# Fused transformer block: GpSimd forms the gated rough reciprocal of the second attention, VectorE's normalisation has three instructions instead of four

## What is computed

```python
def mla_mixer(h, cos, sin, w_in, q_norm, w_q_b, kv_norm, w_kv_b, w_out):
    u = h @ w_in
    c_q, c_kv, k_rope, z = split(u)
    q = rmsnorm(c_q, q_norm) @ w_q_b        # 16 heads of 64 + 32
    kv = rmsnorm(c_kv, kv_norm) @ w_kv_b    # 16 heads of 64 (keys) + 64 (values)
    ...
    for blk in range(S // 128):
        s = (q_nope . k_nope + q_rope . k_rope) * scale, causal by chunks of 64
        prob = softmax(s)
        outs.append(prob . v)
    o = concatenate(outs)
    return (o * silu(z)) @ w_out
```

## Time and profile before

| | |
|---|---|
| median of 3 runs (lowest, highest) | 2193.37 us (2192.48, 2194.1) |
| profiled execution: its time, its span | 2191.03 us, 2189.2 us |
| mean granted TensorE clock | 0.972 |
| busy, share of the span | PE 94%, DVE 49%, ACT 31%, POOL 48% |
| chain that ended last, by engine | PE 74%, DVE 11%, issue 6%, ACT 4%, POOL 3% |
| MLA attention | 16 steps and the last head, from about 1550 to 1953 us |

### The profile page before, as it was taken

The page is one execution under the profiler, slowest core; times in us unless marked ns, Lnnn a source line. Parts: engine busy times, 40 slices in busy tenths (PEclk is TensorE's granted clock), DMA queues, the critical chain, the costliest instruction groups (busy, mean ns, idle before and its releaser), DMA issues.

```text
span 2189.2 us, 26361 instructions
## 1 busy us (share of the span) xinstructions
PE 2053.5 (94%) x9488; PEld 1655.3 (76%) x9488; DVE 1070.3 (49%) x1189; ACT 672.8 (31%) x1085; POOL 1040.6 (48%) x651
## 2 busy tenths in 40 slices
PE   5999989989999999999999997999899999989996
PEld 3777767877778878878878875887677778768775
DVE  6545554646531211212111258422777888763576
ACT  3345564132221001001000122112466666650312
POOL 1545555423733543543443364333456655653372
PEclk9999999988999999999999998999899999999997
DMA  3100000102211211211111122111000000011122
GB/s 138 50 20 21 20 10 29 49 30 106 96 39 48 72 53 48 67 57 48 54 61 48 48 79 76 39 50 39 30 20 19 19 29 19 19 39 48 39 77 96
DMA packets 31642, 106.65 MB, mean 49 GB/s; under 512 B 3449, under 2 KB 3641, under 8 KB 31577
## 3 DMA queue, kind: packets, MB, share of 16 engines
q1 hardware_dynamic: 27520, 96.14, 13.3%
q10 hardware_dynamic: 4066, 9.74, 1.2%
HBM read 101.51 MB, written 4.26 MB: 48 GB/s over the span
## 4 chain that ended last, share of the span: by engine, by line
PE 74%; DVE 11%; issue 6%; ACT 4%; POOL 3%; ACTq 0%; DVEq 0%; DMA 0%; POOLq 0%
PE ps L225 53%; PE ps L390 4%; PE ps L242 2%; PE ps L254 2%; POOL probs_lo L686 2%; PE ps L630 2%; PE ps L618 1%; PE ps L631 1%; DVE mx L731 1%; DVE h_lo L371 1%; PE ps L637 1%; PE ps L617 1%; PE ps L616 1%; DVE tmp L1777 1%; DVE x L1779 1%
## 5 line engine op out<-in xcount | busy, mean ns | idle before, releaser
L1949 POOL TENSOR_TENSOR w_hi<-w_raw,zero 128x1024 fp32r<-128x1024 f32 (+2 forms) x173 | 322.5, 1864 | 815.7 <-PE ps L225 579.5
L1951 POOL TENSOR_TENSOR w_lo<-w_raw,w_hi 128x1024 fp32r<-128x1024 f32 (+2 forms) x173 | 421.1, 2434 | 13.6
L225 PE MATMUL ps<-h_hi,w_lo 128*128 128x512 f32 x1328 | 333.3, 393 | 5.5 <-DVE x L517 5.1
L225 PE MATMUL ps<-h_hi,w_hi 128*128 128x512 f32 x1328 | 328.0, 389 | 0.0
L225 PE MATMUL ps<-h_lo,w_hi 128*128 128x512 f32 x1216 | 300.4, 389 | 0.0
L225 PEld LDWEIGHTS ps<-h_hi,w_lo 128*128 128x128 f32 x1328 | 248.4, 189 | 60.3 <-issue 9.7
L225 PEld LDWEIGHTS ps<-h_hi,w_hi 128*128 128x128 f32 x1328 | 249.2, 188 | 51.8
L686 POOL TENSOR_TENSOR probs_lo<-probs,mla_p_hi 128x512 fp32r<-128x512 f32 x192 | 191.3, 1016 | 171.2 <-ACT probs L679 169.3
L225 PEld LDWEIGHTS ps<-h_lo,w_hi 128*128 128x128 f32 x1216 | 228.2, 188 | 47.6
L1391 DVE TENSOR_TENSOR tmp<-ps,tmp 128x1024 f32<-128x1024 f32 x22 | 26.9, 1224 | 370.3 <-PE ps L225 363.6
L731 DVE TENSOR_REDUCE mx<-ps 128x1 f32<-128x128 f32 (+1 forms) x192 | 140.9, 755 | 79.0 <-PE ps L662 44.4
(11 more groups left out here) (342 smaller groups left out, 3709.2 us busy)
## 6 DMA issues: line engine op xcount, KB each, us to landing
w_raw<-in_wpack SPq DMA_DIRECT2D x173, 512.0 KB, 3.3
x<-in_xT ACTq DMA_DIRECT2D x16, 512.0 KB, 7.9
out<-result SPq DMA_DIRECT2D x8, 512.0 KB, 2.9
p_raw<-in_pT ACTq DMA_DIRECT2D x1, 1024.0 KB, 4.8
pos_i<-in_pos SPq DMA_DIRECT2D x1, 512.0 KB, 6.3
const_stage<-in_consts SPq DMA_DIRECT2D x1, 404.0 KB, 3.3
vec<-in_vecs SPq DMA_DIRECT2D x1, 284.0 KB, 4.7
mla_q_hi<-c_neg ACTq DMA_DIRECT2D x16, 4.0 KB
```

The lines of the kernel that those rows point to most:

```text
L225: last = nc.tensor.matmul(dst[:, half, :], w[slot][:, kt, :], a[:, i, t], start=(n == 0), stop=(n == total - 1))
L1949: nc.gpsimd.tensor_tensor(w_hi[s][:, kts, :], raw[s][:, kts, :], no_change[:, kts, :], ALU.add).then_inc(w_hi_done, 1)
L1951: nc.gpsimd.tensor_tensor(w_lo[s][:, kts, :], raw[s][:, kts, :], w_hi[s][:, kts, :].bitcast(F32), ALU.subtract)\
```

## The change

1. In MLA, GpSimd computes `rec` = `r` times silu(z) (`gate_pool`), once for each half of each head: behind its low part of piece 6 for the first half and behind that of piece 11 for the second. It waits for its own low part, for `r`, and, before it goes on, for its own product.
2. VectorE's normalisation has three instructions in both attentions: sum times `r`, then (that minus 2) times `rec` in MLA (times `r` in fox), then times the output. The second of them waits for GpSimd's product in MLA.
3. `NORM_BEHIND` puts the three behind the fifth, sixth and seventh maximum. For fox this moves its first instruction from behind the fourth to behind the fifth and its second from the fifth to the sixth.
4. `r` of an odd head lies in rows 64 to 127 instead of 0 to 63, so that it stands on the rows of silu(z).

```diff
-        NORM_BEHIND = {3: (0,), 4: (1,), 5: (2,), 6: (3,)}
+        NORM_BEHIND = {4: (0,), 5: (1,), 6: (2,)}
+        GATE_AFTER = {6: 0, N_PIECES - 1: 1}
...
-            nc.scalar.activation(r0[0:HD, :], ln_sum[0:HD, :], ACT.Exp, scale=-1.0).then_inc(A.r0_done, 1)
+            nc.scalar.activation(r0[HD * b:HD * b + HD, :], ln_sum[0:HD, :], ACT.Exp, scale=-1.0).then_inc(A.r0_done, 1)
+
+        def gate_pool(pool, A, n, b, half, tile, g):
+
+            pool.wait_ge(A.p_lo_done, n * N_PIECES + (g + 3))
+            pool.wait_ge(A.r0_done, n * 2 + (half + 1))
+            rows = slice(HD * b, HD * b + HD)
+            z = flat(mix[rows, bass.ds(tile, 1), half * HALF:(half + 1) * HALF])
+            nc.gpsimd.tensor_tensor(rec[rows, :], r0[rows, :], z, ALU.mult).then_inc(A.gate_done, 1)
+            pool.wait_ge(A.gate_done, n * 2 + (half + 1))
...
             if part == 0:
                 dve.wait_ge(A.r0_done, n * 2 + (half + 1))
-                nc.vector.tensor_tensor(sums, sums, r0[0:HD, :], ALU.mult).then_inc(A.newton, 1)
+                nc.vector.tensor_tensor(sums, sums, r0[rows, :], ALU.mult).then_inc(A.newton, 1)
             elif part == 1:
                 dve.wait_ge(A.newton, seq + 1)
-                if again and not gate:
+                if gate:
+                    dve.wait_ge(A.gate_done, n * 2 + (half + 1))
+                elif half == 1 or not (isinstance(n, int) and n == 0):
                     dve.wait_ge(A.norm_done, n * 2 + half)
-                nc.vector.scalar_tensor_tensor(sums if gate else factor, sums, -2.0, r0[0:HD, :], ALU.add, ALU.mult).then_inc(A.newton, 1)
-            elif part == 2 and gate:
+                nc.vector.scalar_tensor_tensor(rec[rows, :], sums, -2.0, (rec if gate else r0)[rows, :], ALU.add, ALU.mult)\
+                    .then_inc(A.newton, 1)
+            elif part == 2:
                 dve.wait_ge(A.newton, seq + 2)
-                if again:
-                    dve.wait_ge(A.norm_done, n * 2 + half)
-                nc.vector.tensor_tensor(factor, sums, dst, ALU.mult).then_inc(A.newton, 1)
-            elif part == 3:
-                dve.wait_ge(A.newton, seq + count)
-                nc.vector.scalar_tensor_tensor(dst, out, -1.0, factor, ALU.mult, ALU.mult).then_inc(A.norm_done, 1)
+                nc.vector.scalar_tensor_tensor(dst, out, -1.0, rec[rows, :], ALU.mult, ALU.mult).then_inc(A.norm_done, 1)
...
                         for g in range(N_PIECES):
                             low_pool(pool, A, n - 1, g)
+                            if A is mla and g in GATE_AFTER:
+                                gate_pool(pool, A, n - 1, 1 - b, GATE_AFTER[g], turn - (b == 0), g)
...
                 for g in range(N_PIECES):
                     low_pool(pool, A, A.heads - 1, g)
+                    if A is mla and g in GATE_AFTER:
+                        gate_pool(pool, A, A.heads - 1, 1, GATE_AFTER[g], last, g)
```

More of the change, by code:

```diff
@@ L554, in __init__ @@
                 self.newton = sem(f"{k}_newton")
+                self.gate_done = sem(f"{k}_gate_done")
                 self.norm_done = sem(f"{k}_norm_done")
@@ L687, in low_pool, with rough_act @@
                 .then_inc(A.p_lo_done, 1)
-        def rough_act(act, A, n, half):
+        def rough_act(act, A, n, b, half):
             act.wait_ge(A.pv_done, n * N_PIECES + (LAST_OF_HALF[half] + 1 + 4))
@@ L695, in rough_act @@
             act.wait_ge(A.ln_done, n * 2 + (half + 1))
-            nc.scalar.activation(r0[0:HD, :], ln_sum[0:HD, :], ACT.Exp, scale=-1.0).then_inc(A.r0_done, 1)
+            nc.scalar.activation(r0[HD * b:HD * b + HD, :], ln_sum[0:HD, :], ACT.Exp, scale=-1.0).then_inc(A.r0_done, 1)
[6 more added lines that the diff above has]
+            pool.wait_ge(A.gate_done, n * 2 + (half + 1))
         def norm_half_dve(dve, A, n, b, half, tile, gate, part):
-            count = 3 if gate else 2
-            seq = n * (2 * count) + half * count
+            seq = n * 4 + half * 2
             rows = slice(HD * b, HD * b + HD)
@@ L704, in norm_half_dve @@
             dst = flat(mix[rows, bass.ds(tile, 1), half * HALF:(half + 1) * HALF])
-            factor = rec[rows, :] if gate else rec[0:HD, :]
-            again = half == 1 or not (isinstance(n, int) and n == 0)
             if part == 0:
                 dve.wait_ge(A.r0_done, n * 2 + (half + 1))
-                nc.vector.tensor_tensor(sums, sums, r0[0:HD, :], ALU.mult).then_inc(A.newton, 1)
+                nc.vector.tensor_tensor(sums, sums, r0[rows, :], ALU.mult).then_inc(A.newton, 1)
             elif part == 1:
                 dve.wait_ge(A.newton, seq + 1)
-                if again and not gate:
+                if gate:
+                    dve.wait_ge(A.gate_done, n * 2 + (half + 1))
+                elif half == 1 or not (isinstance(n, int) and n == 0):
                     dve.wait_ge(A.norm_done, n * 2 + half)
-                nc.vector.scalar_tensor_tensor(sums if gate else factor, sums, -2.0, r0[0:HD, :], ALU.add, ALU.mult).then_inc(A.newton, 1)
-            elif part == 2 and gate:
+                nc.vector.scalar_tensor_tensor(rec[rows, :], sums, -2.0, (rec if gate else r0)[rows, :], ALU.add, ALU.mult)\
+                    .then_inc(A.newton, 1)
+            elif part == 2:
                 dve.wait_ge(A.newton, seq + 2)
-                if again:
-                    dve.wait_ge(A.norm_done, n * 2 + half)
-                nc.vector.tensor_tensor(factor, sums, dst, ALU.mult).then_inc(A.newton, 1)
-            elif part == 3:
-                dve.wait_ge(A.newton, seq + count)
-                nc.vector.scalar_tensor_tensor(dst, out, -1.0, factor, ALU.mult, ALU.mult).then_inc(A.norm_done, 1)
+                nc.vector.scalar_tensor_tensor(dst, out, -1.0, rec[rows, :], ALU.mult, ALU.mult).then_inc(A.norm_done, 1)
         def norm_whole_dve(dve, *which):
-            for part in range(4):
+            for part in range(3):
                 norm_half_dve(dve, *which, part)
@@ L822, in step_act @@
                 if g == 6 and prev is not None:
-                    rough_act(act, A, prev, 0)
+                    rough_act(act, A, prev, 1 - b, 0)
             if prev is not None:
-                rough_act(act, A, prev, 1)
+                rough_act(act, A, prev, 1 - b, 1)
             max_row_act(act, A, n, b, turn)
@@ L835, in last_act @@
                     split(g - (N_PIECES - 2))
-            rough_act(act, A, A.heads - 1, 1)
+            rough_act(act, A, A.heads - 1, 1, 1)
             if split is not None:
```

2 lines of the change are left out of this document (1 added, 1 removed).

## The result

| | before | after |
|---|---|---|
| median of 19 runs each, same chip | 2192.86 us (2188.09 to 2196.9) | 2197.34 us (2195.2 to 2201.68) |
| ratio | | 1.0022, 95% interval 1.0016 to 1.0029 |
| profiled execution, span | 2191.03, 2189.2 us | 2197.77, 2196.0 us |
| VectorE, GpSimd busy | 1070 and 1041 us | 1048 and 1082 us |

The change makes the kernel slower by 3.5 to 6.4 us, 4.5 by the medians. The prediction had the direction, but its +10.0 is more than twice the size.

A forecast was written before the change was run, and what follows sets the result against it. The prediction took TensorE, waiting at each MLA step's end for GpSimd's last low part, as the bound. Terms 7.6 + 0 + 0 + 0.3 + 2.1 = +10.0 us on the median 2193.37 gave 2203, range 2195 to 2208.

The forecast's parts named there:

- What bounds the kernel: At an MLA step's end, TensorE's last value matmul already waits for GpSimd's low part of piece 11.
- both arms: GpSimd's low part of piece 11 and VectorE's eighth maximum, said to arrive together in odd steps; GpSimd has 0.25 room in even.
- Part 1: GpSimd's first-half product behind piece 6: takes 1.27, makes piece 7 0.80 late and piece 11 0.62 late; +7.6 us.
- the dearer case: Rival: product at 1.5 or dear waits, piece 8's low part late too, TensorE stalls twice a step; +13 to +16, chance 0.13.
- 8 x 0.62 + 7 x 0.37 = +7.6: Loss in MLA steps from GpSimd's lateness: 0.62 us in each of 8 odd steps, 0.37 in each of 7 even.
- Part 2: VectorE's first half in MLA: four instructions become three, but the eighth maximum is not earlier; 0.
- at the same distance from the fifth: Sign of being right: the eighth maximum keeps its distance from the fifth maximum in MLA steps.
- Part 3: Second half in MLA: the product, the split queued behind it and VectorE's earlier normalisation change nothing; 0.
- Part 4: Fox: the first normalising instruction moves behind the fifth maximum, idle ahead of the seventh swallows most; +0.3 us.
- Part 5: Last head and behind it: the split queues behind the product, collides with VectorE's low parts of `mix`, TensorE waits; +2.1 us.
- VectorE was the bound: Rival: VectorE's second-half work sets the step time, so 15 x 0.72 = 10.8 us would go: 2182.6; chance 0.04.
- The half-time product: Rival: GpSimd's product on half the partitions takes 0.65, steps cost 0, the end about 1.3; +1.6 us, 2195, chance 0.12.

The follow-up runs named there:

- run 4: Kernel after, with VectorE's three first-half instructions behind the fourth to sixth maximum instead of the fifth to seventh: 2195.93 us, ratio 1.0018.
- run 5: Kernel before, with only the first half's fourth normalising instruction moved from behind the seventh to behind the eighth maximum: 2185.5 us, ratio 0.997.
- run 7: Kernel before, with all four first-half instructions one maximum later, behind the fifth to eighth, and no product on GpSimd: 2194.03 us, ratio 1.0005.
- run 1: Kernel after, but MLA's first half normalised by VectorE alone with four instructions as before; GpSimd multiplies only for the second half: 2193.27 us, ratio 1.0005.
- run 2: Kernel after, but the last MLA head's second half normalised by VectorE alone, without GpSimd's product there: 2195.68 us, ratio 1.0014.
- run 9: Kernel after, last head's second half normalised by VectorE alone, but GpSimd still makes an unused product (r0 times r0) there: 2196.62 us, ratio 1.0019.
- run 3: Kernel after, with one more GpSimd product (r0 times r0) ahead of the first half's product in every MLA head: 2215.47 us, ratio 1.0107.

## Why the prediction was right or wrong

- **What bounds the kernel: this is the step that failed.** I wrote that in the odd step both arms arrive together and that TensorE's last value matmul waits for GpSimd. Lateness did pass one for one from there to the value transposes, but the step did not end by them. I took 0.94, the distance from the value transposes to the transpose of the maxima, for TensorE's own; it is 0.80. And I read the room at the transpose and not at the next step's first matmul, where the odd step has 0.38 more of it. The room was 0.45 and 0.56, where I had 0.25 and 0.
- **Part 1, the product.** 1.29 for 1.27, waits of 0.27 and 0.16 for 0.22 and 0.15, piece 7 0.91 late for 0.80, piece 11 0.68 for 0.62: right and slightly small. The new wait for piece 7's low part was not in the sum (the dearer case had one, for piece 8's), though it makes 0.55 of TensorE's 0.68. **The term "8 x 0.62 + 7 x 0.37 = +7.6" was mis-sized**: between the first matmuls of steps an even step lost 0.24 and an odd one 0.31, where I had 0.37 and 0.62, and all 15 intervals lost 3.9. GpSimd's arm alone is 2.1 of it; the rest is the late eighth maximum (run 4). So the +3.9 comes in about equal parts from the arm that I named and from the one that I had ruled out.
- **Part 2**, the eighth maximum is not earlier for the instruction that goes: right, and runs 4, 5 and 7 show why: it was the wrong one of four. But "at the same distance from the fifth" is wrong: 6.14 before, 6.46 after in the odd step.
- **Part 3**, 0 for the second half: right (run 1).
- **Part 4**, fox +0.3: 0.6, as 0.2 in every other interval and nothing in the rest. In those the gap of the earlier trace rows swallowed less.
- **Part 5**, +2.1 with 0.32 of it in the last head: the tail cost 2.0 and the last head 0.2. Runs 2 and 9 show the cause: the split behind the product, which then stands beside VectorE's low parts.
- **The rivals.** "VectorE was the bound" had 0.04 and a wrong place: not the second half, but the eighth maximum, which the chain of waits named. The first evidence of the profile was right, and I argued it away with a second view. That the time still came out in the stated range is luck in part: the sum was more than twice the loss, and half of the steps' loss has a cause that it did not hold. The half-time product is out at 1.29.

## What to carry to other kernels

Before a step is said to be ended by one engine, take the same distance in several places: the shortest one seen is the most that the engine's own work can need, and what a step has above it is room. Where a chain of waits names an engine, look for what of that engine's work can go behind the thing awaited; that needed one changed number here and gave 7 us, while taking an instruction over to another engine gave nothing. A helping engine with "50% load" is not free in the place that matters, and what its queue holds behind the new work is late too, and so is what the engine that waits for it delivers to a third.

## What was not expected of the hardware

- **The branch is paid from the wait on.** At the loop's end the next matmul came 0.51 to 0.52 behind the end of the maximum that TensorE had waited for, wherever the other work stood (before, after, run 4); at the half-way point without a branch it was 0.14. Behind step 1, where TensorE enters the loop and does not jump back, it was 0.24 (1577.49 to 1577.73 in before). That the branch itself takes the time is read from this; no run changed it alone.
- **An operand used twice is cheaper on GpSimd**: r0 times r0 took 1.04 us (runs 3 and 9), r0 times z 1.29, the same 64 x 512. Where the second operand lies differs too, so that it is the double use is likely and not shown.
- **In the tail VectorE pays, not GpSimd.** In the kernel before the split's two instructions took 2.87 and 2.38, in the kernel after 1.90 and 3.25; together 5.25 and 5.15. GpSimd loses nothing by moving, VectorE's six go from 7.41 to 9.63. `w_lo` ends 2.25 behind the end of VectorE's first low part (1960.60), beside which it had started, and VectorE's second ends 1.08 behind `w_lo`'s: which fits each waiting for the other's end.
- **VectorE's place between its own instructions.** In odd steps of the kernel before the eighth maximum follows the fourth normalising instruction; with the third in its place (run 7) it ends 0.3 later relative to the step's start, though both take 0.7. The rows have it in the joints: in before the fourth instruction starts 0.08 ahead of the seventh maximum's recorded end and the eighth maximum 0.07 ahead of its, in run 7 each starts 0.03 behind. Why is not resolved.
- **TensorE's clock** gave back 1.6 us in the traces. Behind the MLA part the stretch to the end is 227.0 in before and 225.1 in after. The granted clock in windows of 5 us, of before and of after, each at the same distance from the start of unit U_MO + 1 (columns: window; busy and count of PE, PEld, DVE, ACT, POOL; clock; DMA):

```profile
2042.00:2047.00 5.00, 4.85 (x30) 3.98 (x30) 2.39 (x3) 2.94 (x4) 1.04 (x1) 1.00 0.34 105
2047.00:2052.00 5.00, 5.00 (x17) 3.98 (x15) 1.59 (x8) 1.03 (x1) 0.00 (x0) 0.66 0.00 0
```

```profile
2050.70:2055.70 5.00, 4.85 (x30) 4.02 (x29) 2.39 (x3) 2.90 (x4) 1.00 (x1) 1.00 0.32 105
2055.70:2060.70 5.00, 5.00 (x23) 3.98 (x22) 1.56 (x8) 1.35 (x2) 0.28 (x1) 1.00 0.00 0
```

  At 0.66 some two thirds of that window ran at the lower level, 1.2 instead of 2.4 GHz, and the stretch in which it lies is 1.6 longer (22.94 against 21.32 from TensorE's wait for `ssq`, 81.91 behind the start of unit U_MO + 1, to its next wait). The work there is the same, and TensorE was busy ahead of it in both. The stretch is 225 in the profiles of the kernel after and of runs 1, 7 and 9, and 227 in the others; whether it belongs to the kernel or to the execution, single profiles can't say. If it belongs to the kernel, it explains why the stretches add up to more than the medians show.
- **The same dip of 3.4 us moves in the tail.** In all twelve traces the clock is at its upper level from the second transpose of the maxima to the last one, and in the tail once at the lower. In before that lies 0.9 to 4.3 us behind the last value matmul, ahead of TensorE's wait for tile 2, which swallows it; in after 0.2 to 3.6, no dearer. In run 7 it lies 6.1 to 9.5 behind, where no wait follows: matmuls of tile 2 and on come every 0.43 us instead of 0.23, and the tail is 1.4 longer with the same work. In runs 3 and 4 it lies there too, but ahead of the wait for tile 3, and their tail is the 16.7 of after.
